# Expert choice and gate stages: half an early activation ahead of the key scores in four heads, and the tokens' gates moved between one-hots

## What is computed

```python
def peer(hn, w_q, sub_keys, u_emb, v_emb):
    q = (hn @ w_q).reshape(B, T, PEER_HEADS, 2, PEER_HALF)          # 8 heads, 2 x 128
    s = jnp.einsum('bthpd,hpkd->bthpk', q, sub_keys)                # key scores, 128 keys each
    s_top, i_top = lax.top_k(s, PEER_TOPK)                          # 16 and 16
    cand = s_top[..., 0, :, None] + s_top[..., 1, None, :]
    cand_idx = i_top[..., 0, :, None] * PEER_KEYS + i_top[..., 1, None, :]
    best, pos = lax.top_k(cand.reshape(B, T, PEER_HEADS, n_cand), PEER_TOPK)
    experts = jnp.take_along_axis(cand_idx..., pos, axis=-1)
    gates = jax.nn.softmax(best, axis=-1)
    ...
        a = jax.nn.gelu(jnp.einsum('nd,nkd->nk', xc, u_emb[ec]))
        return jnp.einsum('nk,nkd->nd', gc * a, v_emb[ec])
```

## Time and profile before

| | |
|---|---|
| median of 3 runs | 4460.0 us |
| profiled execution | 4461.13 us, its span 4459.3 us |
| TensorE busy | 97% of the span, 84% of the chain that ended last |
| VectorE, ScalarE, GpSimd busy | 62%, 41%, 17% |
| mean granted TensorE clock | 0.991 of full |
| DMA | 142 GB/s over the span |

### The profile page before, as it was taken

One profiled execution on the slowest core, in us unless ns is written; L12 is line 12 of the kernel. 1 busy time (PEld: TensorE's weight loads), 2 busy tenths in 40 slices (PEclk: granted clock), 3 DMA queues, 4 the chain that ended last, 5 costly groups with the idle time before them and its releaser, 6 DMA issues.

```text
span 4459.3 us, 62363 instructions
## 1 busy us (share of the span) xinstructions
PE 4341.5 (97%) x21945; PEld 3656.2 (82%) x21945; DVE 2779.6 (62%) x4610; ACT 1820.3 (41%) x3051; POOL 771.2 (17%) x783
## 2 busy tenths in 40 slices
PE   8999999999999999999999998999999899999998
PEld 7888888888888887888888886787777788888887
DVE  5436557454444436567454368754678888888888
ACT  3223737432232325556332233343326644444444
POOL 1000000000000000000000000010486644444443
PEclk9999999999999999999999999999999999999999
DMA  3222221122222222211222222022223699999997
GB/s 130 97 101 85 95 91 42 67 95 95 103 87 102 94 94 95 103 59 47 85 94 94 104 88 95 1 96 75 82 88 154 253 343 349 341 344 340 343 345 295
DMA packets 93610, 634.52 MB, mean 142 GB/s; under 512 B 13344, under 2 KB 13728, under 8 KB 22752
## 3 DMA queue, kind: packets, MB, share of 16 engines
q1 hardware_dynamic: 58464, 412.95, 25.2%
q0 software_dynamic: 33792, 193.75, 11.8%
q10 hardware_dynamic: 1152, 25.17, 1.3%
HBM read 604.56 MB, written 27.26 MB: 142 GB/s over the span
## 4 chain that ended last, share of the span: by engine, by line
PE 84%; DVE 5%; DMA 3%; issue 2%; DVEq 2%; ACT 2%; POOLq 1%; POOL 0%; ACTq 0%; SPq 0%
PE PB L193 24%; PE PB L195 24%; PE PB L194 23%; PE PB L2795 3%; PE PB L1003 2%; PE PB L3120 2%; DMA UV<-rows,IDX 1%; PE PB L993 1%; DVE WL L3387 1%; DMA RAW<-weights 1%; PE PB L3135 1%; PE PB L1259 1%; PE PB L2308 1%; POOLq L256 1%; DVE PRODG L3370 1%
## 5 line engine op out<-in xcount | busy, mean ns | idle before, releaser
L193 PE MATMUL PB<-XH,WH 128*128 128x512 f32 (+1 forms) x3288 | 1253.6, 381 | 26.5 <-DVE WL L174 14.2
L195 PE MATMUL PB<-XH,WL 128*128 128x512 f32 (+1 forms) x3288 | 1233.8, 375 | 0.0
L194 PE MATMUL PB<-XL,WH 128*128 128x512 f32 (+1 forms) x3288 | 1233.0, 375 | 0.0
L174 DVE TENSOR_TENSOR WL<-RAW,WH 128x1024 fp32r<-128x1024 f32 x520 | 625.7, 1242 | 503.2 <-ACT WH L166 462.8
L193 PEld LDWEIGHTS PB<-XH,WH 128*128 128x128 f32 x3288 | 620.5, 189 | 136.9 <-issue 21.4
L166 ACT ACTIVATE WH<-RAW 128x1024 fp32r<-128x1024 f32 x504 | 506.2, 1049 | 510.3 <-PE PB L195 481.3
L194 PEld LDWEIGHTS PB<-XL,WH 128*128 128x128 f32 x3288 | 621.7, 189 | 99.4 <-issue 2.2
L195 PEld LDWEIGHTS PB<-XH,WL 128*128 128x128 f32 x3288 | 619.6, 188 | 100.5
L254 POOL TENSOR_TENSOR SQ<-SQ 128x512 f32<-128x512 f32 x49 | 72.5, 1480 | 2543.4 <-ACT SQ L236 2521.2
L3387 DVE TENSOR_TENSOR WL<-RAW,WH 128x1024 fp32r<-128x1024 f32 x220 | 269.1, 1223 | 87.9 <-ACT WH L3314 78.7
L193 PE MATMUL PB<-WH,WGH 128*128 128x512 f32 x768 | 301.2, 392 | 11.1 <-DVE WGL L3403 11.1
(11 more groups left out here) (451 smaller groups left out, 7160.1 us busy)
## 6 DMA issues: line engine op xcount, KB each, us to landing
RAW<-weights SPq DMA_DIRECT2D x381, 1024.0 KB
gate_matrix<-STG ACTq DMA_DIRECT2D x4, 4096.0 KB, 12.3
GM<-gate_matrix POOLq DMA_DIRECT2D x128, 128.0 KB
RAW<-weights SPq DMA_DIRECT2D x12, 512.0 KB, 3.9
gate_matrix<-STG ACTq DMA_DIRECT2D x3, 2048.0 KB, 7.4
GM<-gate_matrix POOLq DMA_DIRECT2D x128, 48.0 KB
UV<-rows,IDX POOLq DMA_INDIRECT x160
X<-x SPq DMA_DIRECT2D x4, 512.0 KB, 8.2
```

The lines of the kernel that those rows point to most:

```text
L174: c.nc.vector.tensor_tensor(c.WL[p][:, cols], c.RAW[p][:, cols], c.WH[p][:, cols].bitcast(F32), ALU.subtract).then_inc(c.sem("w_split"), 1)
L193: c.nc.tensor.matmul(out, wh, xh, start=start, stop=False)
L194: c.nc.tensor.matmul(out, wh, xl, start=False, stop=False)
L195: return c.nc.tensor.matmul(out, wl, xh, start=False, stop=stop)
```

## The change

Two parts. In the choice, heads that are neither first nor have turns (2 to 5, those in the loop) run `pe_early` of half 0 ahead of the wait for `pq_ready` and the key scores, and half 1 behind them as before. The order of ScalarE, VectorE, GpSimd and SyncE stays as it was.

In the gates, the one-hots are in one tile `HOT` of eight. Of the first token's pair, ScalarE's one-hot of the second key now carries the gate g: relu(-g (i - k)^2 + g), with scale -g from a new table `NGT`, and bias g from `GTT`. VectorE makes three gated one-hots of the first key (tokens 1 to 3) and one tensor_tensor makes three plain ones: the first key of token 0 and the second keys of tokens 1 and 2. Their keys stand side by side in `PLAIN`, laid over constants that are no longer used. ScalarE fills `NGT` and `PLAIN` with three more activations at the end of the choice. TensorE's matmuls have the same shapes.

```diff
--- before.py
+++ after.py
@@ -1923,6 +1923,8 @@
         with ExitStack() as s:
             c.NORM_PEER = Norm(c.sb("XNP", [P, DC, S], F32, s), None, c.NORM_MEM.RB)
             c.IT1, c.IT2, c.GTT = (c.sb(n, [P, DENSE + 8], F32, s) for n in ("IT1", "IT2", "GTT"))
+            c.NGT = c.sb("NGT", [P, GROUPS], F32, s)
+            c.PLAIN = c.CT[:, CONSTS["ones_head"][0]:]
             with ExitStack() as q:
                 c.RI1, c.RI2, c.RGT = (c.sb(n, [P, QB, P], F32, q) for n in ("RI1", "RI2", "RGT"))
                 c.QP = c.sb("QP", [P, 2, S], F32, q)
@@ -1941,8 +1943,7 @@
                 c.BF = [c.sb(f"BF{i}", [P, 2, QB, TOPK], F32, q) for i in range(2)]
                 c.EQ = c.sb("EQ", [P, QB, TOPK, TOPK], F32, q)
             with ExitStack() as q:
-                c.OA = [c.sb(f"OA{i}", [P, 4, P], F32, q) for i in range(2)]
-                c.OB = [c.sb(f"OB{i}", [P, 4, P], F32, q) for i in range(2)]
+                c.HOT = [c.sb(f"HOT{i}", [P, 8, P], F32, q) for i in range(2)]
                 c.HS = [c.sb(f"HS{i}", [P, P], F32, q) for i in range(2)]
                 c.HP = [c.PR2[:, PRM2[n][0]:PRM2[n][0] + P] for n in ("dw_w", "cmp_w2k")]
                 c.STG = [stage, c.sb("STG1", [P, KEYS, TOK_BLOCK], F32, q)]
@@ -2816,6 +2817,9 @@
             pe.wait_ge(c.sem("early_kept"), tile.k * 2 + 2)
         for n in turns:
             pe_turn_chunk(c, pe, n, 6 + n % 2)
+        fill = not first and not turns
+        if fill:
+            pe_early(c, pe, tile.k * 2, 1 - HEAD_P, (T_CHOOSE + 1) // 2 * 16 + tile.k * 16 + 16, 0)
         pe.wait_ge(c.sem("pq_ready"), tile.k + 1)
         pe.wait_ge(c.sem("ps_scores"), tile.k + 1)
         for m in range(2):
@@ -2826,7 +2830,7 @@
         last.then_inc(c.sem("key_scores"), 1)
         if first:
             pe.wait_ge(c.sem("nx_ready"), (LAYERS + 2) * DC)
-        for half in range(2):
+        for half in range(1 if fill else 0, 2):
             if turns:
                 pe.wait_ge(c.sem("turn_copied"), turns[half] + 3)
             pe_early(c, pe, tile.k * 2 + half, 1 - HEAD_P, (T_CHOOSE + 1) // 2 * 16 + tile.k * 16 + 16, half)
@@ -2942,6 +2946,11 @@
     act.wait_ge(c.sem("turned"), 1)
     for n, dst in enumerate((c.IT1, c.IT2, c.GTT)):
         c.nc.scalar.activation(dst[:, :DENSE], c.PB[:, n, :DENSE], ACT.Copy)
+    c.nc.scalar.activation(c.NGT[:, :], c.PB[:, 2, :DENSE].rearrange("p (g q) -> p g q", q=4)[:, :, 0], ACT.Copy, scale=-1.0)
+    plain = c.PLAIN[:, :GROUPS * 3].rearrange("p (g q) -> p g q", q=3)
+    first, second = (c.PB[:, n, :DENSE].rearrange("p (g q) -> p g q", q=4) for n in range(2))
+    c.nc.scalar.activation(plain[:, :, 0:1], first[:, :, 0:1], ACT.Copy)
+    c.nc.scalar.activation(plain[:, :, 1:3], second[:, :, 1:3], ACT.Copy)
     phase_end(c, act, cur)
 
 
@@ -3090,6 +3099,7 @@
 
 
 GROUPS = DENSE // 4
+HOT_FIRST, HOT_SECOND = (3, 0, 1, 2), (6, 4, 5, 7)
 BLOCKS = DENSE // TOK_BLOCK - 1
 HALVES = DENSE // (TOK_BLOCK // 2) - 2 * BLOCKS
 PER_BLOCK = TOK_BLOCK // 4
@@ -3117,8 +3127,8 @@
     pe.wait_ge(c.sem("hot_pool"), group + 1)
     pe.wait_ge(c.sem("gm_copied"), group + 1)
     for q in range(4):
-        last = c.nc.tensor.matmul(tokens_inside(c, j)[:, :, q], c.OA[j][:, q, :], c.OB[j][:, q, :],
-                                  start=True, stop=True)
+        last = c.nc.tensor.matmul(tokens_inside(c, j)[:, :, q], c.HOT[j][:, HOT_FIRST[q], :],
+                                  c.HOT[j][:, HOT_SECOND[q], :], start=True, stop=True)
     last.then_inc(c.sem("gm_full"), 1)
 
 
@@ -3147,7 +3157,8 @@
     def hot(j, group):
         A.activation(c.HS[j][:, :], c2(c, "iota"), ACT.Square, scale=-1.0, bias=c.IT2[:, bass.ds(group * 4, 1)])
         act.drain()
-        A.activation(c.OB[j][:, 0, :], c.HS[j][:, :], ACT.Relu, scale=-1.0, bias=c.ONES[:, 0:1])\
+        A.activation(c.HOT[j][:, HOT_SECOND[0], :], c.HS[j][:, :], ACT.Relu,
+                     scale=c.NGT[:, bass.ds(group, 1)], bias=c.GTT[:, bass.ds(group * 4, 1)])\
             .then_inc(c.sem("hot_act"), 1)
     hot(0, 0)
     hot(1, 1)
@@ -3199,11 +3210,11 @@
     with dve.Fori(0, GROUPS // 2) as i:
         for j in range(2):
             dve.wait_ge(c.sem("gm_full"), i * 2 + (j + 1))
-            V.tensor_tensor(c.OB[j][:, 1:3, :], iota.unsqueeze(1).to_broadcast([P, 2, P]),
-                            c.IT2[:, bass.ds(i * 8 + (4 * j + 1), 2)].unsqueeze(2).to_broadcast([P, 2, P]), ALU.is_equal)
-            for q in range(4):
+            V.tensor_tensor(c.HOT[j][:, 3:6, :], iota.unsqueeze(1).to_broadcast([P, 3, P]),
+                            c.PLAIN[:, bass.ds(i * 6 + 3 * j, 3)].unsqueeze(2).to_broadcast([P, 3, P]), ALU.is_equal)
+            for q in range(1, 4):
                 tok = i * 8 + (4 * j + q)
-                last = V.tensor_scalar(c.OA[j][:, q, :], iota, c.IT1[:, bass.ds(tok, 1)],
+                last = V.tensor_scalar(c.HOT[j][:, HOT_FIRST[q], :], iota, c.IT1[:, bass.ds(tok, 1)],
                                        c.GTT[:, bass.ds(tok, 1)], ALU.is_equal, ALU.mult)
             last.then_inc(c.sem("hot_dve"), 1)
     dve_split(c, dve, T_PEER, HEAD_P)
@@ -3220,7 +3231,7 @@
             G.tensor_tensor(c.HP[j][:, :], c2(c, "iota"), c.IT2[:, bass.ds(i * 8 + (4 * j + 3), 1)].to_broadcast([P, P]),
                             ALU.subtract)
             pool.drain()
-            G.tensor_scalar(c.OB[j][:, 3, :], c.HP[j][:, :], 0.0, None, ALU.is_equal).then_inc(c.sem("hot_pool"), 1)
+            G.tensor_scalar(c.HOT[j][:, HOT_SECOND[3], :], c.HP[j][:, :], 0.0, None, ALU.is_equal).then_inc(c.sem("hot_pool"), 1)
```

## The result

The changed kernel is slower by a little: 4468.66 us in the median of 14 runs (4464.23 to 4481.44) against 4461.22 us of the kernel before, measured beside it. The ratio is 1.0022, 95% interval 1.0015 to 1.0029, or some 10 us; it compares the means, without one execution of 19648.86 us of the kernel before. The prediction was 4456.7 us. Its sum named a gain of 5.8 us in the choice and a loss of 2.5 us in the gates; the choice gained nothing, and the gates lost more than twice what was worked out.

A forecast was written before the change was run, and what follows sets the result against it. TensorE was taken as the bound, in the gates too. Terms -5.8 + 0.5 + 0 + 2.0 + 0 = -3.3 us turn profiled 4461.1 into 4457.8; less 1.1 to the median, 4456.7. Range 4453 to 4460.5, two in ten outside.

The forecast's parts named there:

- Part 1: Choice: four heads run their first early half before the key scores, saving 1.45 us each, 5.8 us in all.
- The gap: Choice: TensorE idles 1.40 us per head before the key scores; the early half hides ScalarE's 1.02 us query copy fully.
- D: Rival, choice: WL slips over 0.75 us, next tile's weights late; 4458.7 us, chance 0.10. As measured stretch: third STG to last.
- VectorE must be free at T + 9.3: Choice, T the tile's end: VectorE, 20.0 us from WL to BF, ends 7.1 us into the next head, so free.
- GpSimd falls behind by 0.7 a head and costs nothing: Choice: GpSimd's picks need 22.9 us against 22.2 a head; VectorE's resulting 4.6 us delay stays hidden by 8 us slack.
- Part 3: Gates: VectorE's group 0.15 us shorter with three gated one-hots and a three-wide plain one; TensorE gains 0.
- Parts 2 and 4: Choice's end: three more activations, net +0.5 us. Gates: ScalarE's Relu takes its scale from a tile, +2.0 us.
- The start, B: Stretch from the pick's transposes to the gates' first matmul: three more activations there, net +0.5 us.
- Rival B: Gates: ScalarE becomes the bound, deciding from +0.23 us per group; +3.7 us in all, 4463.7 us, chance 0.08.
- E: Gates' start: TensorE's slow-clock stretch, costing some 1.5 us, could vanish or double; 1.5 us either side, no chance given.

The follow-up runs named there:

- e7: Choice of the kernel before, gates of the changed kernel, but VectorE's three gated tensor_scalars ahead of its three-wide tensor_tensor; ratio 1.0014 to the kernel before.
- e1: Kernel before with only the choice's edit, the whole early half ahead of the key scores in heads 2 to 5; ratio 1.0011.
- e2: Kernel before with only the gates' edit, including the three more activations; ratio 1.0017.
- e5: Kernel before with three of eight k-steps of the early half ahead of the key scores in heads 2 to 5; ratio 0.9994.
- e9: Kernel before with the whole early half ahead of the key scores in heads 2 to 5, and VectorE's WL moved ahead of BF; ratio 1.0004.
- e10: Kernel before with three k-steps ahead of the key scores in heads 2 to 5, and WL moved ahead of BF; ratio 0.9996.
- e11: e5 run again, unchanged, against the kernel before; ratio 0.9993.
- e8: Separate probe kernel running VectorE's and GpSimd's instruction forms alone and side by side; GpSimd's small tensor_tensor 0.37 us alone, 0.68 beside VectorE's three-wide one.
- e6: Kernel before with the whole early half ahead of the key scores in heads 3 and 5 alone; ratio 1.0003.

## Why the prediction was wrong

**Part 1, choice, -5.8 forecast, +0.5 measured: the failing step.** The gap went as worked out, and D's question was the right one: is WL in time? The step that failed is "VectorE must be free at T + 9.3: it takes 20.0 us from WL to BF", with WL at 2.36. I carried both durations over as constants of the instructions. In head 2 WL started at T + 9.2, as worked out, but from there to the end of BF it took 22.9 us instead of 20.0: 1.9 of it is WL's own 4.21, and the short tensor_tensors that make the candidates (CAND) grew too, from 1.1 us together to 2.6. So VectorE was free at 9.7 into the next head instead of 7.1, and WL's first half then took 3.07 instead of 1.23: it was done at T + 13.0 of that head, wanted at T + 11.26, and TensorE stood idle for 1.69. The durations of before were those of one alignment with GpSimd; 3.2 us later WL takes 4.2 to 5.0 and a head of VectorE 23.8 to 24.9 us, more than TensorE's 22.2. I had both engines' timelines, and checked each for its own load, but didn't lay one on the other. D stood among the rivals with a chance of 0.10 and 2 us; its place was right, its cause and size weren't. "GpSimd falls behind by 0.7 a head and costs nothing" didn't come to pass either: it waits for a late BF instead.

**Part 3, three-wide one-hot, 0 forecast, +3.7 measured alone.** It was priced on VectorE's timeline only, with bounds of 0 and 0.28 for VectorE and nothing for the stage. VectorE did get shorter as worked out (it waits 17.1 us for the matmuls now, 4.2 before). The lengthening of GpSimd's partner instruction had no term and no bound, and GpSimd, whose two instructions filled the whole group before (0.57 + 0.16 + 0.58 + 0.17 = 1.48), had no spare time to hide it. e7 shows it from the other side: with the order turned GpSimd's is down to 0.50 and two groups are back at 2.97.

**Parts 2 and 4** held. The start, B, grew by 0.64 against +0.5, though the price of a column in it was a slip: with XH's 0.72 less 0.10 for its pointer and GTT's 0.47, 160 columns cost 0.15 us, that is 0.9 ns a column and not 0.7. The Relu cost 2.25 us in D alone, forecast 2.0, and the sizes 0.10 for the pointer and 46 ns for the register step were measured at 92 and 43 ns. Rival B had the gates slower, by 8.6 us where D measured 5.3, and for another engine than the right one.

**E, the clock.** The first groups took 1.2 us more. The granted clock of after (stretch, us, busy times by engine, clock, DMA share, GB/s):

```profile
3403.00:3404.00 1.00, 1.00 (x6) 1.00 (x6) 0.00 (x0) 0.06 (x1) 0.08 (x1) 0.50 0.00 0
3405.00:3406.00 1.00, 1.00 (x8) 0.79 (x7) 0.81 (x3) 0.92 (x2) 0.80 (x2) 0.82 0.00 0
```

And of before:

```profile
3398.00:3399.00 1.00, 1.00 (x7) 1.00 (x7) 0.50 (x2) 0.32 (x1) 0.39 (x1) 0.61 0.00 0
```

In after it is 0.50, the 1.2 GHz level, until 3405.4, some 6.0 us behind the first matmul, where before it was back at 3398.8, 3.7 us behind. It had also fallen earlier, in the idle time ahead of that matmul, so that the slow stretch is 6.8 us long instead of 3.4: it doubled, which E had named as possible. Neither half of the change alone has this (C is 6.55 in e1 and 6.71 in e2), so one execution doesn't show that it belongs to the change. But it isn't mere chance of the execution either: all three executions with e5's choice have C at 7.57 to 7.82. What decides it stays open.

**What stays open.** After, e1, e9 and e10 have spells in which TensorE waits for WL, and e1's median is 4 us above its stretches. Its executions sort by their mean granted clock: two at 0.991 with a median of 4457.4 us, nine at 0.989 or 0.990 with 4466.3; the kernel before, beside it, had 23 of 35 at 0.991 or above, with 4458.9, and twelve below with 4462.7. So it may be that waits inside the projections cost clock in most executions and not in the profiled one. But e9, which waits longest, had 8 of 11 at 0.991, and e11, with a single wait of 0.99 us, 10 of 11 below: this speaks against it, and no run here isolates the cause. The 3.7 us that the last stretch gave back are open as well: behind the last STG the kernels here take between 922 and 929 us with the same code.

## What to carry to other kernels

A duration read from a trace belongs to the instruction and its neighbours. Before moving a VectorE instruction with two SBUF inputs, or making it longer, lay GpSimd's timeline under VectorE's at the old place and at the new one, and look for lengths of the same instruction that differ (2.00 and 2.66, 2.40 and 2.88 stood in the trace of before, in GpSimd's L3065 and L3070): each can be an engine standing still without an idle time. And move as little as covers the gap: three k-steps hid the copy as well as eight did.

## What the runs showed of the hardware

- VectorE's and GpSimd's large tensor_tensors take turns by whole instructions: 3.3 us each, for 1.2 and 2.3 alone (e8). The profile counts the standing still as busy time; neither "idle" nor the waits show it.
- Even a step of 0.22 us waits out a whole 2.4 us instruction of GpSimd (2.23, e9).
- VectorE's gated tensor_scalar (pointer operands, 128x128) doesn't lengthen GpSimd's small tensor_tensor (0.36 us beside it, 0.37 alone), but is itself longer beside it: 0.43 us, 0.34 alone (e8).
- Two engines can lock: with the instruction that releases GpSimd (BF) right ahead of VectorE's next tensor_tensor (WL), they collided in each head behind the first late one, in after, e1, e5 and e6.
